# A hybrid layer with 32 experts: a ring of nine weight places, and TensorE going by experts in groups of three

## What is computed

```python
logits = t @ w_router + b_router              # 256 tokens, 32 experts
top_v, top_e = lax.top_k(logits, 4); gates = softmax(top_v)
# for each expert e, over the tokens that chose it:
a = minimum(xb @ w_gate[e] + b_gate[e], 7.0)  # 1024 x 1024, float32
b = clip(xb @ w_up[e] + b_up[e], -7.0, 7.0)
hid = a * sigmoid(1.702 * a) * (b + 1)
y = hid @ w_down[e] + b_down[e]
out[tokens] += y * gate
```

## Time and profile before

| what | value |
|---|---|
| three runs | 1397.33, 1401.47, 1409.28 us; median 1401.47 |
| span of the profiled execution | 1396.9 us, 0.4 us under the fastest of the three runs |
| busy share | PE 90%, DVE 29%, ACT 19%, POOL 9% |
| moved by DMA | 458.59 MB, mean 328 GB/s |
| mean granted clock of TensorE | 0.962 |
| the chain that ended last | PE 54%, DMA 34%, DVE 7% |

### The profile page before, as it was taken

How to read it: one execution, slowest core, us unless ns; L and a number is a source line. 1 busy time by engine, 2 the same in 40 slices (tenths; PEclk the granted TensorE clock), 3 DMA queues, 4 the chain that set the end, 5 groups by cost and what they waited for, 6 DMA issues and landing times.

```text
span 1396.9 us, 24933 instructions
## 1 busy us (share of the span) xinstructions
PE 1252.0 (90%) x10197; PEld 555.7 (40%) x10198; DVE 402.7 (29%) x896; ACT 260.1 (19%) x501; POOL 121.0 (9%) x168
## 2 busy tenths in 40 slices
PE   5999898568989999988999889988989999999996
PEld 2445445466654333333333333333333333333432
DVE  1265469817855121111111111111111112111112
ACT  2421432336041111111111111100000101100102
POOL 0211540185000000000000000000000000000000
PEclk9999999769988999999999999999999999999998
DMA  9958010010476999999999999999999699969994
GB/s 354 397 182 316 31 61 30 5 34 31 180 308 254 426 426 428 427 428 427 426 426 426 426 428 427 427 427 425 426 426 420 268 427 426 426 266 426 428 427 179
DMA packets 48135, 458.59 MB, mean 328 GB/s; under 512 B 4417, under 2 KB 4817, under 8 KB 22737
## 3 DMA queue, kind: packets, MB, share of 16 engines
q1 hardware_dynamic: 48080, 457.81, 79.1%
HBM read 456.15 MB, written 1.05 MB: 327 GB/s over the span
## 4 chain that ended last, share of the span: by engine, by line
PE 54%; DMA 34%; DVE 7%; issue 2%; ACT 1%; POOL 1%; DVEq 0%; SPq 0%; POOLq 0%; ACTq 0%
DMA arena<-in_w_up 33%; PE bank L1163 21%; PE bank L1190 8%; PE bank L673 7%; PE bank L1055 2%; PE bank L1124 2%; PE bank L584 2%; PE bank L544 1%; DVE arena L1737 1%; PE bank L1172 1%; DVE arena L2266 1%; DVE arena L2263 1%; DVE arena L2261 1%; DMA arena<-in_x 1%; PE bank L904 1%
## 5 line engine op out<-in xcount | busy, mean ns | idle before, releaser
L1163 PE MATMUL bank<-arena 128*64 128x512 f32 x2176 | 484.6, 595 | 43.7 <-DMA arena<-in_w_up 22.5
L1163 PEld LDWEIGHTS bank<-arena 128*64 128x64 f32 x2176 | 150.1, 136 | 359.3 <-issue 263.9
L1190 PE MATMUL bank<-arena 128*64 128x512 f32 x1088 | 239.2, 592 | 0.0
L2259 DVE TENSOR_SCALAR arena<-bank 128x512 f32<-128x512 f32 x34 | 23.6, 693 | 403.3 <-PE bank L1163 403.3
L1190 PEld LDWEIGHTS bank<-arena 128*64 128x64 f32 x1088 | 75.9, 136 | 140.5 <-issue 138.0
L673 PE MATMUL bank<-arena 128*128 128x512 f32 (+1 forms) x320 | 123.7, 540 | 0.0
L673 PEld LDWEIGHTS bank<-arena 128*128 128x128 f32 x320 | 60.7, 195 | 58.2 <-issue 55.3
L2190 DVE TENSOR_SCALAR arena<-arena 96x64 bf16<-96x64 f32 x35 | 8.8, 251 | 224.6 <-PE bank L1190 224.6
L1133 PE MATMUL bank<-arena 64*128 64x512 f32 x280 | 69.6, 614 | 0.8 <-ACT arena L1552 0.8
L1124 PE MATMUL bank<-arena 128*128 128x64 bf16 x1680 | 62.8, 198 | 1.1 <-DVE arena L2186 1.1
L1124 PEld LDWEIGHTS bank<-arena 128*128 128x128 bf16 x1680 | 62.9, 118 | 1.2 <-DVE arena L2186 1.2
(11 more groups left out here) (352 smaller groups left out, 1029.2 us busy)
## 6 DMA issues: line engine op xcount, KB each, us to landing
arena<-in_w_gate SPq DMA_DIRECT2D x64, 2048.0 KB, 22.5
arena<-in_w_up SPq DMA_DIRECT2D x64, 2048.0 KB, 24.1
arena<-in_w_down SPq DMA_DIRECT2D x64, 2048.0 KB, 22.0
arena<-in_w_ada SPq DMA_DIRECT2D x12, 2048.0 KB, 9.7
arena<-in_wfm SPq DMA_DIRECT2D x20, 512.0 KB, 3.4
arena<-in_wz SPq DMA_DIRECT2D x4, 1024.0 KB, 14.3
arena<-in_w_out SPq DMA_DIRECT2D x2, 2048.0 KB, 8.3
arena<-in_x SPq DMA_DIRECT2D x2, 1024.0 KB, 7.6
```

The lines of the kernel that those rows point to most:

```text
L1163: last = mm(ps[m][64 * c_:64 * c_ + 64, :], xcT[:, k, :], ring[:, 2 * h_ + m, k % 4, 512 * c_:512 * c_ + 512], start=False, stop=(k == KT ...
L1190: last = mm(ps[2][64 * c_:64 * c_ + 64, :], hidT[:, k % 4, 64 * (k // 4):64 * (k // 4) + 64], ring[:, 4 + h_, k % 4, 512 * c_:512 * c_ + 5 ...
L2259: v.tensor_scalar(hid[:, 0], ps[0][:, :], LIMIT, None, ALU.min).then_inc(*L.mark("a"))
```

## The change

The ring gets nine places, six side by side (`ring`) and three elsewhere (`ahead0`, `ahead1`, `ahead2`), the latter partly over `h`, `mix` and the first rows of `rows`. Piece n of expert e goes to place (6 e + n) mod 9 and is read there, so that a place depends on e mod 3. A place comes free when the piece nine before it has been used for the last time: for pieces 0 to 2 of an expert these are pieces 3 to 5 of the expert two before, for pieces 3 to 5 pieces 0 to 2 of the expert before.

So SP and TensorE go by experts, in a loop of ten groups of three experts, with an own form of the code for each of the three. TensorE does the first block of an expert unconditionally and all its further blocks right behind it, in `further_blocks`: under an `If`, a loop of three passes, with a second copy of the block and an `If` in each. The order of the 34 blocks is the same. DVE and ACT keep their loops. TensorE's code now has ten copies of the block, six of them in the loop.

Ahead of the table, SP now issues nine pieces instead of six: piece 0 of expert 0 is issued directly after `w_router`, pieces 1 and 2 behind marks of DVE, and three pieces of expert 1, the last two behind the marks of the router part (`logit`, `hparts`, `rest`, `h`) after which `h` and `mix` are not read any more.

For the layout, `rows` is now a list of four areas, the biases' staging (`bst`, `b_part`), `wr`, `hid` and `passed` lie over constants that are out of use by then, the small tiles of a block (`xcT` to `Sb`) over `gates`, `wout`, `yt` and `mixT` in the ring, and the final sum goes to `final` in the ring instead of to `hm`.

```diff
-    keep = put(0, ("const", NCONST), ("x", 2 * D), ("rows", 4 * D), ("cols", 8 + 20 * 5 + 8),
...
+    e = put(keep, ("mix", 2 * D), ("h", 2 * D), ("hT", KT * 256), ("route", 1500), ("bias", 3 * 512), ("hp", 3 * D))
+    at["ahead2"] = (at["rows"][0] + 2 * D, 4096)
+    at["ahead1"] = (at["h"][0], 4096)
+    e = put(e, ("ahead0", 4096), ("ring", PIECES * 4096))
+    assert at["ahead2"][0] + 4096 == at["h"][0] and at["ahead1"][0] + 4096 == at["route"][0]
...
+        places = [area("ring", 4096 * i, 4096) for i in range(PIECES)] + [area(f"ahead{i}") for i in range(PLACES - PIECES)]
...
-            def piece(n, expert):
+            def piece(n, first, group=0):
 
                 m, c = order[n]
-                src = halves[m][bass.ds(expert, 1), c].rearrange("e p n -> p (e n)")
-                sp.dma_start(ring[:, n].rearrange("p k n -> p (k n)"), src).then_inc(sems(f"in_ring{n}"), 16)
-
-
+                place = (PIECES * first + n) % PLACES
+                src = halves[m][first:E_N:PHASES][bass.ds(group, 1), c].rearrange("e p n -> p (e n)")
+                sp.dma_start(places[place], src).then_inc(sems(f"in_place{place}"), 16)
+
+            piece(0, 0)
+            sp.wait_ge(*L.at("dve", "Oss", 1))
+            piece(1, 0)
+            sp.wait_ge(*L.at("dve", "gdn", 1))
+            piece(2, 0)
             sp.wait_ge(*L.at("pe", "mixT", 0, 1))
-            for n in range(3):
-                piece(n, 0)
+            sp.wait_ge(*L.at("dve", "Yss", 1))
+            piece(0, 1)

             sp.wait_ge(*L.at("pe", "low"))
             piece(3, 0)
...
             sp.wait_ge(*L.at("pe", "m", 1, 1))
             piece(4, 0)
             piece(5, 0)
+            sp.wait_ge(*L.at("pe", "logit", 1))
+            sp.wait_ge(*L.at("act", "hparts", 0, 1))
+            sp.wait_ge(*L.at("dve", "rest", 0))
+            sp.wait_ge(*L.at("pool", "rest", 1))
+            piece(1, 1)
+            sp.wait_ge(*L.at("dve", "h", 1))
+            sp.wait_ge(*L.at("dve", "hparts", 1))
+            piece(2, 1)
 
             L.stage("moe")
 
-            def pieces(blocks, expert):
-                L.begin_turn(blocks)
-                for n in range(PIECES):
-                    sp.wait_ge(*L.at("pe", "piece", n))
-                    piece(n, expert)
+            def last_turn_of(expert):
+
+                return sp.value_load(intab[0:1, bass.ds(expert + BLOCKS, 1)], min_val=1, max_val=BLOCKS - 1)
+
+            def later_pieces(first, group, before):
+
+                for n in range(PLACES - PIECES, PIECES):
+                    sp.wait_ge(*L.at("pe", "piece", n - (PLACES - PIECES), turn=before))
+                    piece(n, first, group)
+
+            def first_pieces(first, group, two_before):
+
+                for n in range(PLACES - PIECES):
+                    sp.wait_ge(*L.at("pe", "piece", n + (PLACES - PIECES), turn=two_before))
+                    piece(n, first, group)
 
             sp.wait_ge(*L.at("dve", "table"))
-            with sp.Fori(1, E_N) as i:
-                pieces(sp.value_load(intab[0:1, bass.ds(i + (BLOCKS - 1), 1)], min_val=1, max_val=BLOCKS - 1), i)
+            later_pieces(1, 0, sp.value_load(intab[0:1, BLOCKS:BLOCKS + 1], min_val=1, max_val=BLOCKS - 1))
+            with sp.Fori(0, GROUPS) as g:
+                last = [last_turn_of(g * PHASES + n) for n in range(PHASES + 1)]
+                for n in range(PHASES):
+                    first_pieces(n + 2, g, last[n])
+                    later_pieces(n + 2, g, last[n + 1])
...
-            def block_of_rows(turn, expert, first=False):
+            def place_of(n, first):
+
+                return (PIECES * first + n) % PLACES
+
+            def weights(n, first):
+
+                return places[place_of(n, first)].rearrange("p (k n) -> p k n", k=4)
+
+            def landed(n, first, group):
+
+                return sems(f"in_place{place_of(n, first)}"), group * (2 * 16) + 16 * ((PIECES * first + n) // PLACES + 1)
+
+            def block_of_rows(turn, first, group, start=False):
...
-                        pe.wait_ge(sems(f"in_ring{2 * h_ + m}"), expert * 16 + 16)
+                        w = weights(2 * h_ + m, first)
+                        pe.wait_ge(*landed(2 * h_ + m, first, group))
...
-            def expert_of(turn):
-                return pe.value_load(intab[0:1, bass.ds(turn - 1, 1)], min_val=0, max_val=E_N - 1)
+            def last_turn_of(expert):
+
+                return pe.value_load(intab[0:1, bass.ds(expert + BLOCKS, 1)], min_val=1, max_val=BLOCKS - 1)
+
+            def further_blocks(before, last, first, group):
+
+                with pe.If(last > before + 1):
+                    with pe.Fori(2, SEQ // SLOT + 1) as k:
+                        with pe.If(last > before + (k - 1)):
+                            block_of_rows(before + k, first, group)
+                L.turn = None
 
             pe.wait_ge(*L.at("in", "b_part", 9))
-            block_of_rows(1, 0, first=True)
+            block_of_rows(1, 0, 0, start=True)
             L.turn = None
             pe.wait_ge(*L.at("dve", "table"))
-            with pe.Fori(2, HALF_E + 1) as i:
-                block_of_rows(i, expert_of(i))
-            L.turn = None
+            last = last_turn_of(0)
+            further_blocks(0, last, 0, 0)
+            before, last = last, last_turn_of(1)
+            block_of_rows(before + 1, 1, 0)
+            further_blocks(before, last, 1, 0)
+            with pe.Fori(0, GROUPS) as g:
+                for n in range(PHASES):
+                    before, last = last_turn_of(g * PHASES + n + 1), last_turn_of(g * PHASES + n + 2)
+                    block_of_rows(before + 1, n + 2, g)
+                    further_blocks(before, last, n + 2, g)
             n_more = pe.value_load(intab[0:1, 80:81], min_val=0, max_val=MAX_MORE)
-            with pe.Fori(0, MAX_MORE) as k:
-                with pe.If(n_more > k):
-                    block_of_rows(k + HALF_E + 1, expert_of(k + HALF_E + 1))
-            with pe.Fori(HALF_E + 1, E_N + 1) as i:
-                block_of_rows(n_more + i, expert_of(n_more + i))
```

More of the change, by code:

```diff
@@ L110, in own, with at @@
         return self.sem, self.n if self.turn is None else self.turn * self.per + self.n
-    def at(self, who, *step, back=0):
+    def at(self, who, *step, back=0, turn=None):
         name, value = self.book.old.get((who,) + step) or self.book.new.get((who,) + step) or (f"{who}_dry", 1)
@@ L116, in at @@
         if name in self.book.per_old:
-            value = (self.turn - back) * self.book.per_old[name] + value
+            value = ((self.turn if turn is None else turn) - back) * self.book.per_old[name] + value
         return self.sems(name), value
@@ L151, in put @@
         return base
[L153 to L154 removed]
+    keep = put(0, ("const", NCONST), ("x", 2 * D), ("cols", 8 + 20 * 5 + 8),
+               ("small", 720), ("gates", 2304), ("rows", 4 * D))
     ops = put(keep, ("kT", 4 * 512), ("qT", 4 * 256), ("bT", 2 * 512), ("cT", 2 * 256), ("k_tm", 4 * 512),
@@ L221, in layer_program @@
         xin = view(area("x"), 2, D)
-        rows = view(area("rows"), 4, D)
+        rows = [area("rows", D * at_, D) for at_ in (2, 3, 1, 0)]
         npm = area("cols", 0, 8)
@@ L336, in layer_program @@
         bias = area("bias").bitcast(BF16).rearrange("p (m d) -> p m d", m=3)
-        acc = view(area("acc"), 2, D)
+        acc = view(area("ring", 0, 2 * D), 2, D)
+        final = view(area("ring", 4096, 2 * D), 2, D)
         xcT = view(area("xcT"), KT, SLOT)
-        hid = view(area("hid"), 6, 512)
+        hid = [area("hid", 512 * i, 512) for i in range(4)] + [area("hid4")]
         hidT = view(area("hidT"), 4, 128)
@@ L445, in _ @@
                 load(f"win{i}", area("win", i * 1024, 1024), wfm[i])
-            load("wrow", area("rows", 0, 3 * D), wrow)
+            load("wrow", area("rows", 2 * D, 2 * D), wrow[:, 0:2 * D])
+            load("wrow", rows[2], wrow[:, 2 * D:3 * D])
             def load_brow(which):
@@ L1065, in _ @@
                     at_ = 2 * (KT * j + k)
-                    last = mm(ps[4][:, at_:at_ + 2], rows[:, row, 128 * k:128 * k + 128], ident[:, 0:2], start=True, stop=True)
+                    last = mm(ps[4][:, at_:at_ + 2], rows[row][:, 128 * k:128 * k + 128], ident[:, 0:2], start=True, stop=True)
             last.then_inc(*L.mark("rcols"))
@@ L1167, in block_of_rows @@
                 pe.wait_ge(*L.at("act", "y", back=1))
-                scatter(first).then_inc(*L.mark("back"))
+                scatter(start).then_inc(*L.mark("back"))
                 pe.wait_ge(*L.at("dve", "hid"))
                 for k in range(4):
-                    last = nc.tensor.transpose(unit(ps[0], k), hid[:, 4, k:512:4], ident)
+                    last = nc.tensor.transpose(unit(ps[0], k), hid[4][:, k:512:4], ident)
                 last.then_inc(*L.mark("hidT"))
@@ L1186, in block_of_rows @@
                 for h_ in range(2):
```

(5 more changed lines are left out.)

61 lines of the change are left out of this document (33 added, 28 removed).

## The result

The changed kernel takes 1464.93 us (median of 4 runs, 1463.22 to 1471.1), the kernel before 1399.4 in the same comparison: ratio 1.0473, 95% interval 1.0421 to 1.0525. It is 4.7% slower. The forecast was 1390. The profiled execution took 1463.36 us, its span is 1461.5 (before: 1396.9).

What follows compares the result with a forecast made beforehand. Weight arrival (29.47 us an expert) was taken to set the pace over TensorE (26.23 us a block), until the second blocks. - 14.7 - 2.8 + 1.4 + 4.5 = - 11.6 us gave 1385.3, 1390 at the median; range 1380 to 1418.

Steps and rivals of the forecast that it cites:

- Code that isn't there: TensorE's longer loop: the long jump back misses its code, 1.5 us each, three after 1060 us, 4.5 us lost.
- Its price: TensorE's missed jump: one packet's 1.06 us plus a start, 2.7 to 4.2 us, less 1.9 of cover: 0.8 to 2.3.
- The skips at nothing: TensorE's jumps over the second form, 1.4 packets forward, taken as free like the short jumps back.
- Those before it cost nothing: the 3.24 us between block and weights hide them: TensorE's long jumps back before 1060 us: hidden, as a block is 3.24 us shorter than its expert's weights.
- The second rival: TensorE's jump over the second form misses at every change of expert, 2.3 us each: 1417 us; chance 0.22.
- Earlier weights: SP's weight queue: three pieces of expert 1 go out before the table, so every later piece lands 14.7 us early.
- The extra blocks: Experts with a second block: nine places keep weights loading, so the 2.8 us wait at 1235 us goes.
- An expert with second blocks: TensorE's inner loop and compares for further blocks: 2.2 us on top, 0.7 x 2 = 1.4 us lost.
- TensorE's own control, added: TensorE's sequencer: one more load, compare and register sums per expert, 1.15 us, nothing while the cover stands.
- the first rival: TensorE's new code is all kept, or its fetches stay under 1.9 us: - 16.1 us, 1385.4; chance 0.30.
- TensorE's cover: TensorE's sequencer runs 3.1 us ahead of its queued matmuls; less 1.15 of new control, 1.9 us remain.
- Third rival: SP's three early pieces bring nothing, held up until after 431.6 us: 1400 to 1404, say 1402; chance 0.12.

Runs made afterwards that it cites:

- the run with a quarter of the bytes: Changed kernel, with SP bringing only 1024 of 4096 columns of each weight piece from expert 2 on; 1414.9 us (one run).
- The first experiment: Changed kernel with the ten groups of experts written out one after the other, so no jump back, skips kept; 1409.06 us, ratio 1.0085.
- the written-out form: Changed kernel with its ten groups written out instead of looped: 1409.06 us with the skips, 1386.19 us without them.
- the written-out kernel: Changed kernel with groups written out and one block form per expert in an inner loop, nothing skipped; 1386.19 us, ratio 0.9906.
- the one-form kernel: Changed kernel, its loop over ten groups kept, with one block form per expert in an inner loop instead of two forms; 1378.44 us, ratio 0.9833.

## Why the prediction was wrong

The step that failed is *Code that isn't there*. It named the mechanism, the place and the condition, the jump back over more than eight packets that no row covers, and the runs bear these out. Three of its terms were off:

- *Its price.* The bounds were 2.7 to 4.2 us for a missed jump, built from one packet's 1.06 us and the start of an 8 KB load. The jump back takes 7.4 us: about 5 on quiet DMA engines (the run with a quarter of the bytes) and 2.7 more on full ones, and two packets are fetched, not one. Its neighbour, the skip ahead of it, takes 5.9 to 6.5 and uses up the sequencer's lead, so nothing hides the second wait. The first experiment shows the skip without the jump, 2.6 us of gap instead of 10.5, and the changed kernel's gap at 1149.54 the jump without the skip: 6.0 us by the sequencer, 4.9 of gap. Forecast were 0.8 to 2.3 us of idle TensorE for each such jump, measured 11.2 for the pair, and some 2 more of slow clock.
- *The skips at nothing*, taken "for the long jump back alone". Every skip in the changed kernel waits, 1.4 to 6.5 us, and the skips were worth 23 us in the written-out form. "No such jump is in the trace" was a slip for the short one: L1207 makes it 13 times, free; the code on which it lands had just run and was still held.
- *"Those before it cost nothing: the 3.24 us between block and weights hide them".* Three experts have 9.7 us of such slack together. From gap to gap, 565.87 to 659.13, three blocks take 93.3 us, 14.6 over 3 x 26.23: the gap, 2.3 of slow clock and the shorter skips. So TensorE falls 4.9 us behind the weights in every group, and the price is paid nine times, not three. That also undoes the gain of the early weights: no wait for weights is left for them to shorten.

The second rival had this arithmetic: beyond 3.24 us an expert TensorE is the bound everywhere, and 3.5 us each gives + 53. The waits measured are 126.3/33 = 3.83 us a block; with 33 x 0.33 more, + 64, and it is + 64.6. That is the account above in other words, no second proof. Its place was only part of it: each expert's skip does wait, but two of three are short, and the jump back is the larger part. On the Trainium skill's rule ("Runtime: NRT & Kernel Launch", Instruction fetch mechanics) that a taken branch out of the current two-page window forces a fetch: in the changed kernel both jumps do so, as the page says; but loops of 4.2, 5.5 and 6.9 packets jump back in 0.22 us, so two pages is not TensorE's window here. The same section gives TensorE an instruction memory of 2048 instructions, 8 packets of 256, and the limit found between 6.9 and 8.2 agrees with that.

The other steps:

- *Earlier weights*: they go out as forecast, by 422 us, and piece 3 at 431.79 (forecast 431.6). SP's timeline after:

```profile
399.36 0.81 SPq L509 DMA_DIRECT2D arena<-in_w_down  x2
415.89 0.33 SPq L509 DMA_DIRECT2D arena<-in_w_up  x1
419.98 0.33 SPq L509 DMA_DIRECT2D arena<-in_w_gate  x1
431.79 0.33 SPq L509 DMA_DIRECT2D arena<-in_w_up  x1
```

  Their worth, 14.7 us, was right: in the kernel where they count, the last wait for weights ends at 1061.93 instead of 1074.59, 12.7 us earlier, although its first part ended later and piece 3 went out only at 433.84, 2.2 us behind the 431.62 of the earlier trace rows. Counted from there it is 14.9. Taking the pieces out of the written-out kernel costs 10.4 to 11.4; why less there is open.
- *The extra blocks*, 2.8 us: from the last wait for weights to the last block's end the one-form kernel gains 15.7 - 12.7 = 3.0 us more. Right, though no run changed that part alone.
- *An expert with second blocks*, 1.4 us lost: nothing of it shows. In the changed kernel the blocks before and behind the second one follow at 26.22 to 26.24 us (1096.85 to 1123.08; 1275.01, 1301.25, 1327.47).
- *TensorE's own control, added*: it costs nothing that shows where the code is held. The one-form kernel carries nearly all of it and came within 0.5 us of the first rival's sum, which has the loads, compares and sums at nothing. So close a hit is partly luck: the later end of its first part (2.2 us) and the 1.4 us that the sum takes off for the second blocks nearly cancel.
- *TensorE's cover*, 3.1 us less 1.15 of new control, 1.9: nearly right, 13.6 of waiting gave 11.2 of idle time, so 2.4 were covered.
- Third rival (the early pieces bring nothing): out, by the run without them.

## What to carry to other kernels

Where code runs in a loop on TensorE, count the instructions of one pass, rare copies that are skipped included, and keep them under what the traces show to be held (here 6.9 packets, 1712 instructions, were and 8.2, 2093, weren't); a rare case is cheaper as another turn of the same form than as a second form that is mostly jumped over. When a cost is off every row of the trace, don't bound it by the smallest transfer that looks like it: ask what the sum does if the cost is three times the bound, and whether the slack that hides one holds for the sum of all of them.

## What the runs showed of the hardware

- TensorE's sequencer keeps the code of the last passes: at most 0.25 us for a jump back over 8.3 packets of which 1.4 were gone through, and over 6.9 all gone through; 6.0 us when 8.2 were gone through. Copies that a short skip passes over are mostly fetched (122 packets against 81).
- A jump back to code that is not held takes 4.7 us with DMA engines busy a third of their time and 6 to 7.6 with full ones, several times the 1.06 us that a packet takes to move. A prefetch hint 85 us ahead saves 1.5 us of 7.4. A skip takes 1.4 to 2.2 us where its packet was on its way already (skip at 507.7, packet from 507.1 on), 5.9 to 6.5 where it starts 3.7 us after the skip (560.8).
- Fetched instructions delay the data: the written-out kernel moves 37 packets more than the looped one (81 against 44), about 39 us of one DMA engine, and its last wait for weights ends at 1066.6 instead of 1061.9 us. The lag grows from 0.7 us at 670 to 4.7 there. They have no other difference but the loop; that the packets are the cause is argued, not shown.
- Behind a gap of 10 to 11 us TensorE's first matmuls run at 1.2 GHz, which costs 1.7 to 3.1 us more. In the first experiment so do those behind ten of twelve gaps of 2.3 to 2.95 us; behind the other two the clock is 1.00.
